# Transformer block stack: router weights as the stationary side, forget gates amid the K banks, merge low halves on GpSimd

## The reference, cut to what matters

```python
# first block
fq = _rms(_heads(proj("fox_q"), FOX_HEADS), fox_q_norm_g[l])
fk = _rms(_heads(proj("fox_k"), FOX_HEADS), fox_k_norm_g[l])
log_f = jax.nn.log_sigmoid(proj("fox_f") + b_forget[l])      # 16 forget gates a token
y_fox = attention(fq, fk, fv, bias = cumsum(log_f) differences, causal)
gates = sigmoid(proj("gates") + b_gate[l])                   # 4 branches x 1024
projected = einsum('bsnc,ncd->bsnd', branches, w_branch[l])
mixed = sum(gates * projected, axis=2)                       # the merge
# second block, two layers, stream x and (layer 0) context
h2 = modulate(rmsnorm(x, g_norm2[i]), sh2, sc2)
aff = softmax(h2 @ w_r)                                      # router: 1024 x 16
gate, idx = top_k(aff.T, 32)                                 # 32 of 256 tokens for each expert
x = x + gt2 * experts(h2, idx, gate)
```

## Time and profile before

| | |
|---|---|
| Median of 3 runs | 2955.91 us (2947.69 to 2959.1) |
| Profiled execution | 2956.62 us, span 2954.8 us, mean granted TensorE clock 0.957 |
| TensorE matmuls | 2573.3 us busy, 15018 records |
| VectorE / ScalarE / GpSimd | 1077.0 / 884.7 / 347.1 us busy |
| DMA | 669.31 MB, mean 227 GB/s |

### The profile page before, as it was taken

One profiled execution on the slowest core, in us unless ns is written; L12 is line 12 of the kernel. 1 busy time (PEld: TensorE's weight loads), 2 busy tenths in 40 slices (PEclk: granted clock), 3 DMA queues, 4 the chain that ended last, 5 costly groups with the idle time before them and its releaser, 6 DMA issues. The chain is left out here.

```text
span 2954.8 us, 37912 instructions
## 1 busy us (share of the span) xinstructions
PE 2573.3 (87%) x15018; PEld 1799.9 (61%) x15018; DVE 1077.0 (36%) x1556; ACT 884.7 (30%) x1398; POOL 347.1 (12%) x185
## 2 busy tenths in 40 slices
PE   7899989999999999899987888887898987788786
PEld 7788877889997678688742222224776982222222
DVE  4447533446754434543430011014455651000001
ACT  4465533344443343422320000002334441000001
POOL 0330003341000221000310000000132020000000
PEclk8999999999999999999989999998998999999999
DMA  4434326664543121322279999996212457999996
GB/s 179 149 133 160 115 86 258 265 224 168 185 157 129 72 68 45 155 100 100 100 282 407 400 405 411 414 407 247 100 59 81 172 219 298 411 393 411 410 409 278
DMA packets 92888, 669.31 MB, mean 227 GB/s; under 512 B 10288, under 2 KB 10464, under 8 KB 12736
## 3 DMA queue, kind: packets, MB, share of 16 engines
q1 hardware_dynamic: 90256, 654.63, 56.9%
q0 software_dynamic: 2208, 11.43, 1.1%
q10 hardware_dynamic: 272, 1.05, 0.1%
HBM read 666.00 MB, written 1.06 MB: 226 GB/s over the span
## 5 line engine op out<-in xcount | busy, mean ns | idle before, releaser
L2429 PE MATMUL ps<-ring,WK 128*64 128x512 f32 x2984 | 703.9, 602 | 151.7 <-DMA ring<-in_stream 128.2
L562 PE MATMUL ps<-A,piece_hi 128*128 128x256 f32 (+1 forms) x1952 | 624.0, 320 | 39.2 <-DVE ring_lo L481 10.9
L563 PE MATMUL ps<-A,piece_hi 128*128 128x256 f32 (+1 forms) x1952 | 610.0, 313 | 0.0
L564 PE MATMUL ps<-A,ring_lo 128*128 128x256 f32 (+1 forms) x1952 | 609.3, 312 | 0.0
L2429 PEld LDWEIGHTS ps<-ring,WK 128*64 128x64 f32 x2984 | 189.3, 136 | 630.6 <-DMA ring<-in_stream 330.0
L481 DVE TENSOR_TENSOR ring_lo<-ring,piece_hi 128x1024 fp32r<-128x1024 f32 x287 | 355.7, 1244 | 381.2 <-ACT piece_hi L472 380.7
L472 ACT ACTIVATE piece_hi<-ring 128x1024 fp32r<-128x1024 f32 x378 | 391.5, 1053 | 265.0 <-DMA ring<-in_stream 120.2
L562 PEld LDWEIGHTS ps<-A,piece_hi 128*128 128x128 f32 x1952 | 382.4, 196 | 82.7 <-issue 48.9
L563 PEld LDWEIGHTS ps<-A,piece_hi 128*128 128x128 f32 x1952 | 382.8, 196 | 18.3
L564 PEld LDWEIGHTS ps<-A,ring_lo 128*128 128x128 f32 x1952 | 381.7, 196 | 18.6
L483 POOL TENSOR_TENSOR ring_lo<-ring,piece_hi 128x1024 fp32r<-128x1024 f32 x91 | 235.8, 2596 | 791.1 <-ACT piece_hi L472 791.1
(11 more groups left out here) (271 smaller groups left out, 2683.6 us busy)
## 6 DMA issues: line engine op xcount, KB each, us to landing
ring<-in_stream SPq DMA_DIRECT2D x610, 1024.0 KB, 7.6
WK<-in_ahead SPq DMA_DIRECT2D x5, 1024.0 KB, 9.2
WK<-in_na_bias POOLq DMA_DIRECT2D x2, 2048.0 KB, 7.8
hi_place<-in_ahead SPq DMA_DIRECT2D x4, 1024.0 KB, 12.8
WK<-cum_scratch POOLq DMA_DIRECT2D x1, 2048.0 KB, 11.7
A_place<-in_ahead SPq DMA_DIRECT2D x2, 1024.0 KB, 17.2
const<-in_const SPq DMA_DIRECT2D x1, 1235.0 KB, 10.5
WK<-in_x SPq DMA_DIRECT2D x1, 1024.0 KB, 5.2
```

Source lines behind the costliest of these rows:

```text
L562: nc.tensor.matmul(out_, l[0], r[0], start=first, stop=False)
L563: nc.tensor.matmul(out_, l[0], r[1], start=False, stop=False)
L564: return nc.tensor.matmul(out_, l[1], r[0], start=False, stop=last)
L2429: last = nc.tensor.matmul(ps[64 * n:64 * n + 64, bank, :], lhs, piece[:, n * 512:n * 512 + 512], start=(k == 0), stop=(k == DC - 1))
```

## The change

Three parts. (1) The router's weights are padded to 32 columns and become the stationary side; HF streams, 128 tokens a matmul, and token tile m writes partitions 32m to 32m+31 of one bank. VectorE copies the logits to LOGITS, TensorE turns them back. One bank of token rows for each token tile goes into the middle of the k loop, two behind the logits, the rest behind the affinities; the order of the rows changes with it. (2) The forget logits come after four of the eight K banks; VectorE's and ScalarE's parts move with them, and the second half of VectorE's part, the sum, gets its own place. (3) All of pieces 88 to 151 get their low half from GpSimd.

```diff
-    for lo, hi in ((24, 40), *((block + l * layer + 12, block + l * layer + 32) for l in range(LAYERS)),
+    for lo, hi in ((24, 40), (88, 152), *((block + l * layer + 12, block + l * layer + 32) for l in range(LAYERS)),
...
-    GPS_LOW[split[89:152:2]] = True
...
         def qk_pe(pe, cur, ready):
...
-            fm_banks(pe, cur, in_a()(T), T, DC)
+            fm_banks(pe, cur, in_a()(T), T, DC // 2)
+            forget_pe(pe, cur)
+            fm_banks(pe, cur, in_a()(T), T, DC // 2)
...
-            for h in range(2):
-                copies(eng, who, cur, lambda j, h=h: KT[:, 4 * h + j, :], 4, T)
+            behind()
+            copies(eng, who, cur, lambda j: KT[:, j, :], 4, T)
+            forget()
+            copies(eng, who, cur, lambda j: KT[:, 4 + j, :], 2, T)
+            gates()
+            copies(eng, who, cur, lambda j: KT[:, 6 + j, :], 2, T)
...
-        ROWS_FIRST = 3
+        ROWS_FIRST = 2
+        LOGITS = wk(5632, P)
...
                 for m in range(tt):
-                    last = nc.tensor.matmul(ps[:, b, 16 * m:16 * m + 16], HF[:, k, m * P:(m + 1) * P], wr[:, k, :],
-                                            start=(k == 0 and m == 0), stop=(k == DC - 1 and m == tt - 1))
+                    last = nc.tensor.matmul(ps[32 * m:32 * m + 32, b, 0:P], wr[:, k, :], HF[:, k, m * P:(m + 1) * P],
+                                            start=(k == 0), stop=(k == DC - 1))
+                if k == 3:
+                    for i in range(tt):
+                        token_rows(i)
                 if ada and k in step:
                     ada_pe(pe, cur, 1, step[k])
...
-            for i in range(ROWS_FIRST):
+            pe.wait_ge(bank_free[b], logits_read)
+            bank_parts(pe, cur, [(P, 0, 32 * tt, [(LOGITS[0:32 * tt, :], ident[0:32 * tt, 0:32 * tt])])], turn=True)
+            for i in range(tt, tt + ROWS_FIRST):
                 token_rows(i)
             if ada:
                 ada_pe(pe, cur, 1, 11)
...
+            for i, (m, h) in enumerate(row_order(tt)):
+                if i == 2:
+                    act.wait_ge(aff_logits, cur.base("route") + 1)
+                    nc.scalar.activation(AFF[:, 0:tt, :], AFF[:, 0:tt, :], ACT.Exp).then_inc(aff_exp, 1)
...
+            read_bank(dve, cur, True, lambda bank: nc.vector.tensor_copy(LOGITS[0:32 * tt, :], bank[0:32 * tt, 0:P]))
...
-            head_norm_act(act, cur, steps, fox_norm, after_squares=lambda: forget_act(act, cur, steps),
+            head_norm_act(act, cur, steps, fox_norm,
```

More of the change, by code:

```diff
@@ L1258, in qk_pe, with qk_read @@
             fm_banks(pe, cur, in_a()(T), T, DC - 3)
-            fm_banks(pe, cur, in_a()(T), T, DC)
+            fm_banks(pe, cur, in_a()(T), T, DC // 2)
+            forget_pe(pe, cur)
+            fm_banks(pe, cur, in_a()(T), T, DC // 2)
         def v_pe(pe, cur, kv=0):
             tm_tile(pe, cur, kv, TT)
-        def qk_read(eng, who, cur, beside):
+        def qk_read(eng, who, cur, beside, behind, forget, gates):
             for c in range(DC):
@@ L1294, in forget_dve, with gates_dve @@
             dve.drain().then_inc(fox_z, 1)
+        def gates_dve(dve, steps):
             dve.wait_ge(fox_e, 1)
@@ L2241, in build, with row_order @@
         UNIT = wk(5376, T)
-        ROWS_FIRST = 3
+        ROWS_FIRST = 2
+        LOGITS = wk(5632, P)
+        def row_order(tt):
+            return [(m, h) for h in range(2) for m in range(tt)]
         def route_pe(pe, cur, st, ada):
             tt = 2 * st
-            wr = p2("w_router", 0, DC * 16).rearrange("p (k e) -> p k e", k=DC)
+            wr = p2("w_router", 0, DC * 32).rearrange("p (k e) -> p k e", k=DC)
             step = {-1: 8, 3: 9, 5: 10}
@@ L2255, in route_pe, with token_rows @@
                 ada_pe(pe, cur, 1, step[-1])
+            logits_read = cur.bank_use(1)
+            cur.g += 1
+            def token_rows(i):
+                m, h = row_order(tt)[i]
+                bank_parts(pe, cur, [(P, c * P, P, [(HF[:, 4 * h + c, m * P:(m + 1) * P], ident)])
+                                     for c in range(4)], turn=True)
             for k in range(DC):
@@ L2276, in route_pe @@
             bank_parts(pe, cur, [(64, m * P, P, [(AFFW[:, m, :], ident)]) for m in range(2)], turn=True)
-            for i in range(ROWS_FIRST, 2 * tt):
+            for i in range(tt + ROWS_FIRST, 2 * tt):
                 token_rows(i)
@@ L2308, in route_act @@
             tt = 2 * st
-            act.wait_ge(aff_logits, cur.base("route") + 1)
             skip_banks(cur, 1)
-            nc.scalar.activation(AFF[:, 0:tt, :], AFF[:, 0:tt, :], ACT.Exp).then_inc(aff_exp, 1)
-            for i in range(2 * tt):
-                if i == ROWS_FIRST:
+            for i, (m, h) in enumerate(row_order(tt)):
+                if i == 2:
+                    act.wait_ge(aff_logits, cur.base("route") + 1)
+                    nc.scalar.activation(AFF[:, 0:tt, :], AFF[:, 0:tt, :], ACT.Exp).then_inc(aff_exp, 1)
+                if i in (tt, tt + ROWS_FIRST):
                     skip_banks(cur, 1)
-                m, h = i // 2, i % 2
                 read_bank(act, cur, True, lambda bank, m=m, h=h: nc.scalar.activation(
@@ L2320, in route_act @@
                     nc.scalar.activation(H2_HI[:, m, :], H2[m], ACT.Copy).then_inc(h2_hi, 1)
+            if tt == ROWS_FIRST:
+                skip_banks(cur, 1)
             skip_banks(cur, 1)
@@ L2742, in _ @@
             main_norm_act(act, cur, steps, 2 * T, streams=1)
[L2743 to L2747, removed]
+            qk_read(act, "act", cur, beside=lambda c: norm_hi_act(act, cur, c, 1, None, True), behind=lambda: None,
+                    forget=lambda: skip_banks(cur, 1), gates=lambda: forget_act(act, cur, steps))
+            qk_written(act, cur)
             act.wait_ge(x_lo, cur.base("x"))
-            head_norm_act(act, cur, steps, fox_norm, after_squares=lambda: forget_act(act, cur, steps),
+            head_norm_act(act, cur, steps, fox_norm,
                           ahead=lambda: v_read(act, "act", cur, 0), between=lambda: next_piece(act, cur, 2),
@@ L2851, in _ @@
             main_norm_dve(dve, cur, steps, 2 * T, gain, streams=1, between=first_lows)
-            qk_read(dve, "dve", cur, beside=lambda c: second_chunk_dve(dve, cur, c, gain, None))
-            second_chunk_dve(dve, cur, DC, gain, None)
-            forget_dve(dve, cur, steps)
+            qk_read(dve, "dve", cur, beside=lambda c: second_chunk_dve(dve, cur, c, gain, None),
+                    behind=lambda: second_chunk_dve(dve, cur, DC, gain, None),
+                    forget=lambda: forget_dve(dve, cur, steps), gates=lambda: gates_dve(dve, steps))
             head_norm_dve(dve, cur, steps, fox_norm, ahead=lambda: v_read(dve, "dve", cur, 0),
```

15 lines of the change are left out of this document (5 added, 10 removed).

## The result

The changed kernel takes 2922.53 us (median of 4 runs, 2920.89 to 2923.55) beside 2957.27 us of the kernel before in the same runs: ratio 0.9894, 95% interval 0.9875 to 0.9914, where 31.1 us less were forecast. The ratio makes that 31 us, the two medians 34.7, and the spans of the two profiled executions, 2921.7 and 2954.8, 33.2.

The account below looks back on a forecast made before the run. TensorE, busy 87% of the span, was taken to lose time where it stands still or runs slowly. Terms -9.8 (forget gates), -13 (merge), -6 and -2.3 (routers) sum to -31.1, from 2956.6 to 2925.5 us; range 2910 to 2948.

Parts of the forecast that it names:

- so its two reads and the masks move by as much: First projections, GpSimd: with gates 9.7 us earlier, reads and masks also end 9.7 earlier, at 117.
- The rule on the shared ports: Merge: GpSimd and two-SBUF-input VectorE instructions lock one port pair, so the later waits; 2.56 us waiting assumed per product bank.
- Group ends: Merge, ends of modulation groups: without VectorE's low half, 20.4 us becomes 15.6 twice (-4.8 each), the last 16.0 becomes 12.8 (-3.2).
- Steady pairs: Merge, pairs between group ends: 7.34 us a pair against 7.42, about -1.5 us over 22 pairs.
- the round of 14.7 us: Merge: weight slot's closed chain from use through reload and GpSimd's low half, 14.7 us for two pairs.
- By the rule or without it the sum stays: Merge: even with port waits VectorE needs 6.8 us a pair, under the round's 7.3, so -13 us holds.
- Rival 1: Merge: low half in the chain, VectorE not returning slots late; rounds 1.33 us longer, bubbles stay: 2953 us, chance 0.12.
- rival 2: Merge: ring hides nothing; each pair pays 1.33 us plus 0.4 from locked ports: 2976 us, chance 0.05.
- Rival 5: Steady merge pairs fall to 6.98 us (-8), clock stays up at barrier and router (-5): 2912 us, chance 0.13.
- 0.49 us a K block: Router, layer 0: four column tiles of one k take 0.49 us, bounds 0.25 and 1.75.
- rival 3: Router: layer 0's gain ends at loads, or records stay near 0.2 us; -1 in each layer: 2932 us, chance 0.13.
- 8 x 0.25: Router, layer 1: eight K blocks at 0.25 us bring 6.98 us of records to 2.0.

Follow-up runs that it names:

- the order run: Kernel before, low halves unmoved; in block one's merge ScalarE gives back product-bank pieces, VectorE's last low half goes behind ROWS and the gate signal: merge 248.26 us, ratio 0.9928.

## Why the prediction was right

The sum came out nearer than its parts. By stage the forget gates gave 1.6 us less than forecast, the router of layer 0 2.9 more and that of layer 1 1.7 less; these nearly cancel.

**Forget gates (-9.8, measured -8.2 in the stage).** TensorE's share and ScalarE's were as worked out: gates made from 80.92 to 84.78, ahead of GpSimd's 86.5 (86.3 forecast), and TensorE waits 3.03 us, "near 3". That number is luck: TensorE ended 1.5 us later than forecast and the barrier opened 1.3 later. The step that was off is "so its two reads and the masks move by as much". The reads got 2.7 us shorter, so the masks start at 104.6 and not "near 107.5", and the masks 4.15 longer, since at their new place they meet three of VectorE's instructions; apart from the COPY they took 9.39. The rule on the shared ports was weighed at the merge and not here, where it bore.

**Merge (-13, measured -13.1).** The sum is closer than its terms. Group ends, from slice to slice: -4.8, -4.4 and -3.2, forecast -4.8, -4.8, -3.2 (the first went from 21.1 to 16.3 us, not from 20.4 to 15.6: the stretch of the earlier trace rows starts 1.7 us behind the slice). First pair: -1.3 for +1.3, and that is the clock. Steady pairs: +0.7 over the stage for -1.5; the round of 14.7 us was right, but the old pace was 7.31 and not 7.42, which came from the same badly placed stretch. Without the luck of the clock the part is worth 11 to 12. The mechanism, give-back in VectorE's queue order, is shown by the order run. What the prediction did not see: the order alone is worth 18, so GpSimd was the dearer cure; and the 2.17 us of the earlier trace rows already was a cost of the kernel before. "Makes nearly every such addition wait" was wrong: with twice the low halves on GpSimd 12 of the 32 additions were held up and not 16, and the mean fell from 1180 to 774 ns. "By the rule or without it the sum stays" held for this change, and hid a gain beside it. Rival 1 is half true: the low half is in the chain, as the 7.35 us a pair show, but VectorE did give the slots back late. Its +14.6, and rival 2, fall with every merge run. Rival 5's pace of 6.98 came only with the new order.

**Router, layer 0 (-6, measured -8.9).** 0.49 us a K block was near enough: blocks start 0.43 apart at the lower clock and 0.22 at the full one. The term that was mis-sized is what stands around them: slices and transposes were priced at the lower level, as in the kernel before, but here the clock was at its upper level, 2.4 GHz, from about the first transposes on (0.79 over the ten us from 1451.4, with TensorE busy throughout them but for 0.5 us). From the first router matmul to the logits it took 7.3 us and not 11.4, and from there to the top-k 3.2, not 5.4. (The prediction's own terms, 4.7 + 1.3 - 0.9, make 5.1.) So the top-k gained 12.5 for 5.6. The loads did follow, but not whole, as rival 3 had it in kind: 3.4 us stayed there.

**Router, layer 1 (-2.3, measured -0.6).** "8 x 0.25" took the full clock, but at the lower one the blocks start 0.43 us apart. Four profiles with this code gave -0.6 to -0.7 and one, where the clock rose earlier, -3.2; the size of this part hangs on the clock, which the prediction did not weigh here.

**No cost beside.** Nothing of the 32 low halves given to GpSimd, nor of the wider parameter rows, shows in another stage beyond the scatter.

## What to carry to other kernels

Where a buffer is given back by the engine that reads a result, look at what stands ahead of that read in its queue: a short operation whose input is still under way holds it as long as a long one. Reordering was worth more here than moving the work to another engine, 18.3 us of the merge against 11.2. And whatever is moved onto GpSimd, or in time, is to be checked for VectorE's instructions beside it; before a load that someone will wait for, look which loads are queued ahead that nobody needs yet.

## What was not expected of the hardware

VectorE's COPY, with one SBUF input, took 3.24 us beside GpSimd's masks and 2.29 alone, and a low half 3.35 and 1.22. The section of the Trainium skill cited above (SBUF — State Buffer, "SBUF: two separate sides") names, beside two SBUF inputs, VectorE's two-port modes; in which mode the COPY ran no run here shows. It did write its 4096 elements a partition at 0.56 ns each, where a low half takes 1.19 each, which would fit such a mode. A K block of the router took as long with two column tiles as with four: they start 0.43 us apart at the lower clock. The same code in layer 1's router got its full clock 5.8 or 9.0 us after the stage's start, from one profile to the next, worth 2.5 us of a stage of 35.
